# A hybrid decoder layer on one core: the last down tile split at token 256, and the closing norm's vectors in PSUM

## The reference

```python
x = layer_norm(ALPHA * x + merged @ w_out, ln1_g, ln1_b)
f = (jax.nn.silu(x @ w_ff_gate) * (x @ w_ff_up)) @ w_ff_down
x = layer_norm(ALPHA * x + f, ln2_g, ln2_b)
```

## Time and profile before

| what | value |
|---|---|
| median of three runs | 979.53 us (978.2, 979.53, 979.75) |
| the profiled execution, its own time | 978.52 us |
| its span, first to last instruction | 976.7 us |
| TensorE matmul busy | 937.5 us (96% of the span), granted clock 0.987 of full on average |
| VectorE busy | 612.2 us (63%) |
| ScalarE busy | 380.1 us (39%) |
| GpSimd busy | 368.5 us (38%) |
| DMA | 89.35 MB, mean 91 GB/s |

### The profile page before, as it was taken

The page is one execution under the profiler, slowest core; times in us unless marked ns, Lnnn a source line. Parts: engine busy times, 40 slices in busy tenths (PEclk is TensorE's granted clock), DMA queues, the critical chain, the costliest instruction groups (busy, mean ns, idle before and its releaser), DMA issues.

```text
span 976.7 us, 18914 instructions
## 1 busy us (share of the span) xinstructions
PE 937.5 (96%) x7382; PEld 932.4 (95%) x7382; DVE 612.2 (63%) x929; ACT 380.1 (39%) x593; POOL 368.5 (38%) x286
## 2 busy tenths in 40 slices
PE   6979999999999999999999999999999999999993
PEld 6979999999999999999999998999999999999992
DVE  2796979795302898543344689977878778321216
ACT  3423232324636333333222446555455457222211
POOL 3735565647354454444345453000000003433413
PEclk9989999999999999999999999999999999999996
DMA  8523232322322323322334230433433433432202
GB/s 240 152 63 96 86 95 86 86 65 75 97 66 66 98 66 96 97 84 78 97 101 125 66 87 1 130 87 98 117 86 89 125 86 101 139 93 86 60 1 92
DMA packets 166658, 89.35 MB, mean 91 GB/s; under 512 B 4634, under 2 KB 164674, under 8 KB 166609
## 3 DMA queue, kind: packets, MB, share of 16 engines
q1 hardware_dynamic: 164377, 87.75, 31.3%
q10 hardware_dynamic: 2232, 0.92, 0.4%
HBM read 85.49 MB, written 3.17 MB: 91 GB/s over the span
## 4 chain that ended last, share of the span: by engine, by line
PE 82%; DVE 13%; SPq 2%; issue 1%; ACT 1%; DMA 1%; DVEq 0%
PE main L1079 52%; PE main L1313 18%; PE main L1229 4%; PE aux L1313 3%; DVE aux L1547 2%; PE aux L1079 2%; PE aux L1065 1%; SPq L429 1%; DVE x_sum L1901 1%; DMA ln_tok<-in_ln_b 1%; DVE merged L1770 1%; DVE merged L1725 1%; DVE main L1722 0%; DVE glu_pad L1558 0%; DVE aux L1528 0%
## 5 line engine op out<-in xcount | busy, mean ns | idle before, releaser
L532 POOL TENSOR_TENSOR w_lo<-raw,w_hi 128x1024 fp32r<-128x1024 f32 (+1 forms) x128 | 280.6, 2196 | 554.6 <-ACT w_hi L654 552.5
L1079 PE MATMUL main<-x_hi,w_lo 128*128 128x272 f32 x1024 | 213.5, 290 | 6.5 <-DVE dch_pad L1572 5.0
L1079 PE MATMUL main<-x_hi,w_hi 128*128 128x272 f32 x1024 | 212.9, 289 | 0.0
L1079 PE MATMUL main<-x_lo,w_hi 128*128 128x272 f32 x1024 | 212.1, 289 | 0.0
L654 ACT ACTIVATE w_hi<-raw 128x1024 fp32r<-128x1024 f32 x128 | 135.2, 1058 | 146.2 <-PE main L1079 139.8
L1079 PEld LDWEIGHTS main<-x_hi,w_lo 128*128 128x128 f32 x1024 | 161.9, 189 | 7.2 <-POOL w_lo L532 5.2
L1079 PEld LDWEIGHTS main<-x_lo,w_hi 128*128 128x128 f32 x1024 | 161.8, 190 | 0.0
L1079 PEld LDWEIGHTS main<-x_hi,w_hi 128*128 128x128 f32 x1024 | 160.8, 190 | 0.0
L1079 PE MATMUL main<-y,w_hi 128*128 128x272 f32 x512 | 84.6, 287 | 0.0
L1547 DVE SCALAR_TENSOR_TENSOR aux<-glu_pad,miscT,aux 128x512 f32<-128x512 f32 x112 | 75.2, 751 | 0.0
L1079 PEld LDWEIGHTS main<-y,w_hi 128*128 128x128 f32 x512 | 72.1, 188 | 0.0
(11 more groups left out here) (366 smaller groups left out, 2128.4 us busy)
## 6 DMA issues: line engine op xcount, KB each, us to landing
raw<-in_w_in SPq DMA_DIRECT2D x64, 512.0 KB, 4.1
raw<-in_w_ff_gate SPq DMA_DIRECT2D x22, 512.0 KB, 4.0
raw<-in_w_ff_up SPq DMA_DIRECT2D x22, 512.0 KB, 5.0
raw<-in_w_branch SPq DMA_DIRECT2D x32, 256.0 KB, 3.5
raw<-in_w_ff_down SPq DMA_DIRECT2D x16, 512.0 KB, 4.0
raw<-in_w_out SPq DMA_DIRECT2D x8, 512.0 KB, 3.9
raw<-in_w_ff_down SPq DMA_DIRECT2D x8, 384.0 KB, 3.4
x_tok<-in_x_prompt SPq DMA_DIRECT2D x4, 512.0 KB, 6.4
```

The lines of the kernel that those rows point to most:

```text
L532: pool.tensor_tensor(w_lo[s][:, 0:n, :], raw[s][:, 0:n, :], w_hi[s][:, 0:n, :].bitcast(F32), ALU.subtract).then_inc(w_lo_ready, 1)
L1079: mm = pe.matmul(ps[:, h, :], w[s][:, k, :], x[:, h * HALF:(h + 1) * HALF], start=(first and k == 0 and j == 0), stop=(last and k == n - 1 ...
```

## The change

Two edits meet in the last 35 us.

*The split.* The last tile is made in two unequal parts, given by a table `LAST`: first tokens 256 to 544 (288 columns: token tiles 2, 3 and the samples), then tokens 0 to 256 (tiles 0 and 1). A new function `turn_last(n)` turns a part; that of the first part, with the samples, comes 12 matmuls into the second instead of 24. `half_unit` is no longer called here. The first residual step now writes back to the matmul's own PSUM bank and not to `S[2]`. VectorE takes `row_statistics(KD - 2)` ahead of the first residual, and finishes in another order: the samples and half of tile 2, the residual of the second part, the rest of tile 2, the second statistics, tile 0, the left half of tile 1. ScalarE and GpSimd take tile 3, and then the right half of tile 1. The output DMAs are in a new order.

*The vectors.* ScalarE copies `g_row` to `g_ps` (`main` banks 0 and 1) and `b_row` to `b_ps` (`aux` banks 2 and 3) once these banks are free, and `finish` reads `g_ps` and `b_ps`. GpSimd still reads `g_row` and `b_row`.

```diff
+        g_ps = main[:, 0:2, :].rearrange("p a n -> p (a n)")
+        b_ps = aux[:, 2:4, :].rearrange("p a n -> p (a n)")
+        LAST = ((2, NTILE + 1, 2 * P, NT), (0, 2, 0, 2 * P))
...
-                    (rows_ready, 1, o_x[:, 0, :], r_tok[:, 0, :]), (pool_rows, 2, o_x[:, 1, :], r_tok[:, 1, :]),
-                    (rows_ready, 2, o_x[:, 2, :], r_tok[:, 2, :]),
-                    (pool_rows, 4, o_x[:, 3, D // 2:D], r_tok[:, 3, D // 2:D]),
-                    (rows_ready, 3, o_s, rs_tok[:, :]),
-                    (rows_ready, 4, o_x[:, 3, 0:D // 2], r_tok[:, 3, 0:D // 2]))):
+                    (rows_ready, 1, o_s, rs_tok[:, :]), (rows_ready, 3, o_x[:, 2, :], r_tok[:, 2, :]),
+                    (pool_rows, 2, o_x[:, 3, :], r_tok[:, 3, :]), (rows_ready, 4, o_x[:, 0, :], r_tok[:, 0, :]),
+                    (pool_rows, 4, o_x[:, 1, D // 2:D], r_tok[:, 1, D // 2:D]),
+                    (rows_ready, 5, o_x[:, 1, 0:D // 2], r_tok[:, 1, 0:D // 2])):
...
-            for n, (j, cols) in enumerate(((1, slice(0, D)), (3, slice(D // 2, D)))):
+            for n, (j, cols) in enumerate(((3, slice(0, D)), (1, slice(D // 2, D)))):
...
+            act.wait_ge(row_vecs, 32)
+            act.wait_ge(tile_out[0], T_DOWN + KD // 2 + 1)
+            act.activation(g_ps, g_row[:, :], ACT.Copy).then_inc(vecs_copied, 1)
+            act.wait_ge(rows_out, KD - 1)
+            act.activation(b_ps, b_row[:, :], ACT.Copy).then_inc(vecs_copied, 1)
+            for n, (j0, j1, c0, c1) in enumerate(LAST):
+                act.wait_ge(rows_turned, KD + n)
+                ins = act.activation(r_tok[:, j0:j0 + 2, D - P:D],
+                                     aux[:, 1 - n, 0:2 * P].rearrange("p (j n) -> p j n", j=2), ACT.Copy)
+                if n == 0:
+                    ins = act.activation(rs_tok[:, D - P:D], aux[0:B * T, 1, 2 * P:3 * P], ACT.Copy)
...
+            def turn_last(n):
+
+                c0, c1 = LAST[n][2:]
+                pe.wait_ge(r_ready, 3 * KD + n)
+                pe.wait_ge(rows_out, KD - 2 + n)
+                for j in range(2):
+                    mm = pe.transpose(aux[:, 1 - n, j * P:j * P + P], S[1][:, c0 + j * P:c0 + j * P + P], ident[:, :])
+                if n == 0:
+                    mm = pe.transpose(aux[0:B * T, 1, 2 * P:3 * P], S[1][:, SEQ:NT], ident[:, :])
+                mm.then_inc(rows_turned, 1)
...
+                    for i in range(parts_):
+                        if n == 0 and k + i == DOWN_SPLIT[0]:
                             turn_rows(KD - 2)
+                        if n == 1 and k + i == 4:
+                            turn_last(0)
+                        xh, xl = h_hi(k + i)[:, c0:c1], h_lo[:, k + i, c0:c1]
+                        for t, (w, x) in enumerate(((w_l, xh), (w_h, xl), (w_h, xh))):
+                            mm = pe.matmul(main[:, 2 + n, 0:c1 - c0], w[:, i, :], x,
+                                           start=(k + i == 0 and t == 0), stop=(k + i == KF - 1 and t == 2))
+                    k += parts_
+                mm.then_inc(last_done, 1)
+            turn_last(1)
...
-                ve.scalar_tensor_tensor(S[2][:, cols], x_lo[:, KD - 1, cols].bitcast(F32), ALPHA,
-                                        main[:, 2 + h, 0:HALF], ALU.mult, ALU.add).then_inc(last_out, 1)
+                ve.scalar_tensor_tensor(bank, x_lo[:, KD - 1, c0:c1].bitcast(F32), ALPHA, bank,
+                                        ALU.mult, ALU.add).then_inc(last_out, 1)
...
-                after(link(ve.scalar_tensor_tensor(t, t, bn_mv[0:q, j, 0:1], g_row[0:q, cols],
+                after(link(ve.scalar_tensor_tensor(t, t, bn_mv[0:q, j, 0:1], g_ps[0:q, cols],
                                                    ALU.subtract, ALU.mult)))
-                ve.scalar_tensor_tensor(t, t, bn_rs[0:q, j, 0:1], b_row[0:q, cols], ALU.mult, ALU.add)\
+                ve.scalar_tensor_tensor(t, t, bn_rs[0:q, j, 0:1], b_ps[0:q, cols], ALU.mult, ALU.add)\
                   .then_inc(rows_ready, 1)
...
+            row_statistics(KD - 2)
             residual_last(0)
-            row_statistics(KD - 2)
             ve.wait_ge(bn_zero, 1)
-            last_statistics(0, 0, 2)
-            ve.wait_ge(row_vecs, 32)
+            last_statistics(0, 2, NTILE + 1)
+            ve.wait_ge(vecs_copied, 2)
+            finish(rs_tok[:, :], B * T, NTILE, slice(0, D))
+            finish(r_tok[:, 2, left], P, 2, left)
+            residual_last(1)
+            finish(r_tok[:, 2, right], P, 2, right)
+            last_statistics(1, 0, 2)
             finish(r_tok[:, 0, :], P, 0, slice(0, D))
-            ve.wait_ge(unit_done, U_END)
-            residual_last(1)
-            last_statistics(1, 2, NTILE + 1)
-            finish(r_tok[:, 2, :], P, 2, slice(0, D))
-            finish(rs_tok[:, :], B * T, NTILE, slice(0, D))
-            finish(r_tok[:, 3, 0:D // 2], P, 3, slice(0, D // 2))
+            finish(r_tok[:, 1, left], P, 1, left)
```

More of the change, by code:

```diff
@@ L1404, in _ @@
             pe.wait_ge(tile_out[1], T_DOWN + (KD - 1) // 2 + 1)
-            for h in range(2):
+            for n, (j0, j1, c0, c1) in enumerate(LAST):
                 k = 0
-                for part, n in enumerate(DOWN_SPLIT):
+                for part, parts_ in enumerate(DOWN_SPLIT):
                     u = U_END - 3 + part
-                    if h == 0:
+                    if n == 0:
                         pe.wait_ge(w_lo_ready, u + 1)
-                    mm = half_unit(w_hi[u % RING], w_lo[u % RING],
-                                   [(h_hi(k + j), h_lo[:, k + j, :]) for j in range(n)],
-                                   main[:, 2 + h, 0:HALF], h, first=(part == 0), last=(part == 2))
-                    k += n
-                    if h == 1:
-                        mm.then_inc(unit_done, 1)
-                    elif part == 2:
-                        mm.then_inc(last_half, 1)
-                    if part == 0:
-                        if h == 0:
-                            turn_rows(KD - 2)
-                        else:
-                            pe.wait_ge(r_ready, 3 * KD)
-                            pe.wait_ge(rows_out, KD - 2)
-                            for j in range(2):
-                                mm = pe.transpose(aux[:, 1, j * P:j * P + P], S[1][:, j * P:j * P + P],
-                                                  ident[:, :])
-                            mm.then_inc(rows_turned, 1)
@@ L1429, in _ @@
-            pe.wait_ge(r_ready, 3 * KD + 1)
-            pe.wait_ge(rows_out, KD)
-            for j in range(2, NTILE):
-                pe.transpose(aux[:, 1, j * P:j * P + P], S[1][:, j * P:j * P + P], ident[:, :])
-            pe.transpose(aux[0:B * T, 3, 0:P], S[1][:, SEQ:NT], ident[:, :]).then_inc(rows_turned, 1)
+                    w_h, w_l = w_hi[u % RING], w_lo[u % RING]
+                    for i in range(parts_):
+                        if n == 0 and k + i == DOWN_SPLIT[0]:
+                            turn_rows(KD - 2)
+                        if n == 1 and k + i == 4:
[4 more added lines that the diff above has]
+                                           start=(k + i == 0 and t == 0), stop=(k + i == KF - 1 and t == 2))
```

37 lines of the change are left out of this document (15 added, 22 removed).

## The result

| | before | changed |
|---|---|---|
| median | 978.6 us (6 runs, 975.33 to 979.75) | 972.61 us (6 runs, 970.02 to 974.82) |
| ratio | 1 | 0.994, 95% interval 0.9916 to 0.9964 |
| profiled execution | 978.52, span 976.7 | 974.82, span 973.0 |

The kernel is faster by 0.6%, in the direction and by the way that were forecast, but 972.61 lies 0.19 under the low end of the range (972.8).

The account below looks back on a forecast made before the run. VectorE was taken to bound the last 17.3 us, 3.1 of it waiting for GpSimd. VectorE's end -5.34 and DMA queue +0.44 gave -4.9, from 979.0 to 974.1 us; range 972.8 to 976.5.

Parts of the forecast that it names:

- So I take both as free of each other: Closing norm: VectorE's finish with a PSUM vector and GpSimd don't wait for each other; 1.28 us per instruction of 1024 columns.
- Rival 1: Closing norm: VectorE and GpSimd still wait for each other with vectors in PSUM; 980.7 us, chance 0.02.
- I take nothing for it: VectorE's residual and finishing instructions: reading PSUM instead of SBUF costs no extra time.
- Rival 4: VectorE's eleven instructions newly reading PSUM cost a little more, 0.2 us in all; 974.3 us, chance 0.10.
- The copies: ScalarE's two vector copies into PSUM fit its idle time; 0.8 to 3.0 us for both, cost nothing.
- Rival 2: Last tile's second part: 256-column matmuls run at another rate, 0.23 us each; 980.9 us, chance 0.04.
- -5.34 + 0.44 = -4.9: Whole span: VectorE's end 5.34 us earlier, queueing of the last output DMAs 0.44 later, so 4.9 less.
- with 0.03 between: VectorE's finishing instructions: a gap of 0.03 us between one and the next.
- +1.3 = 971.8: Output DMA tail: the last bytes end at 970.49 and the span 1.3 us later, at 971.8.
- down 1.3 for the runs' spread (978.2 against 979.5): Low side of the forecast range: 1.3 us under 974.1 for run spread and no DMA queue, giving 972.8.
- Rival 5: Last tile: an unseen wait eats the new order's gain, only 3.1 us of GpSimd waiting saved; 975.9 us, chance 0.06.
- rival 3: Output DMA tail: the last three transfers go one after another, 1.7 us later; 975.8 us, chance 0.10.

Follow-up runs that it names:

- E4: Changed kernel without GpSimd's four closing-norm instructions; 28.86 us from the last tile's first matmul to the span's end, against 28.93.
- E7: Changed kernel with the second part's residual ahead of the left half of tile 2; 29.95 us from the last tile's first matmul to the span's end.
- E13: Kernel before plus two small VectorE writes that nobody reads; 33.87 us from the last tile's first matmul to the span's end, against 34.60.
- E1: Kernel before with only the vectors moved to PSUM, its split, order and residual kept; median 974.26 us, ratio 0.9939.
- E3: Kernel before without GpSimd's four closing-norm instructions; 31.18 us from the last tile's first matmul to the span's end, against 34.60.
- E2: Changed kernel with the vectors left in SBUF and no copies, new split and order kept; median 978.4 us, ratio 0.9986.

## Why the prediction was right, and where it wasn't

- **"So I take both as free of each other":** right. E4 puts what is left at 0.07 of stretch. Rival 1 is refuted.
- **"I take nothing for it" (PSUM reads):** right. On 1024 columns 1.27 and 1.28 against 1.28, on 512 0.73 to 0.75 against 0.73 and 0.75. Rival 4 doesn't show in any of the eleven. Nor does the rule of the Trainium skill, "VectorE: DVE Perf Modes", section "The TRN2 errata" (an estimated 0.065 more each); the measurement decides.
- **The copies:** 1.01 and 1.00, between the bounds 0.38 and 1.52, and hidden.
- **The matmuls:** end at 17.42, predicted 17.42. Rival 2 fell: 256 columns take 0.117.
- **VectorE to the first finishing:** starts at 13.93, predicted 13.81; the residual at 17.86 against 17.97. The wait that the new order makes is there (0.44 after the last matmul, predicted 0.55), and E7 shows that to do without it is worse.
- **The sum, "-5.34 + 0.44 = -4.9":** this is the step that failed. The stretch lost 5.67. The mechanism was right, and two terms of the sum had the wrong size, by 0.45 and 0.32:
- **"with 0.03 between":** VectorE's end lies at 25.92, predicted 26.37, so 0.45 too late. I had put 0.03 between all instructions. Where one has no wait of its own it starts some 0.08 before its predecessor's end (968.46 against 967.26 + 1.28 = 968.54), so a pair of 512 columns takes 1.43 to 1.44 instead of 1.51. The earlier trace rows showed it: 971.09 + 1.27 = 972.36, and the next starts at 972.29.
- **"+1.3 = 971.8" (from the last bytes to the end):** predicted 3.33 from VectorE's end, measured 3.01, so 0.32 too long. The queue itself is right: E13, whose code packet comes early, has a tail of 2.52, the changed kernel 3.01, so +0.49 against the predicted +0.44. But the 1.3 of the kernel before held 0.37 that goes with its late code packet, and the changed kernel, with two more VectorE instructions, lost it. I took a row of one kernel as a constant of the chip. That the edit moved the packet was luck.
- **The range:** with both terms as measured the forecast is 974.1 - 0.77 = 973.3 and the low end 972.0, and 972.61 is inside; one of the two alone would have done for the 0.19. The other 0.7 down to 972.61 is scatter of runs, for which "down 1.3 for the runs' spread (978.2 against 979.5)" left little room: my 979.0 for the kernel before came from four executions, and its median beside the experiments lies between 978.6 and 979.8. Three runs showed 1.5 of spread; six of the changed kernel have 4.8, and 17 of the kernel before, run beside E1, have 6.2 (975.56 to 981.8). A spread read from three runs was made into a bound.
- **Rival 5** is refuted by the stretch (5.67 off, and 4.94 by the account below, not 3.1), and rival 3 by the tail.

One more thing that I had read wrongly: part of VectorE's idle 1.56 before the second statistics. TensorE's timeline of the kernel before, and of E13:

```profile
961.66 0.69 PE L1432 MATMUL aux<-ident,scr 128*128 128x128 f32 x2 [2.24 <-DVE scr L1983]
```
```profile
960.10 0.44 PE L1432 MATMUL aux<-ident,scr 128*128 128x128 f32 x2 [2.22 <-DVE scr L1983]
```

Two stretches of the kernel before, and the one of E13 (PEclk is the third number from the end):

```profile
961.00:962.00 1.00, 0.34 (x2) 0.34 (x3) 0.61 (x1) 0.00 (x0) 0.92 (x2) 0.76 0.26 102
962.00:963.00 1.00, 0.56 (x3) 0.08 (x1) 0.00 (x0) 0.40 (x2) 1.00 (x1) 0.50 0.00 0
```
```profile
960.00:961.00 1.00, 0.55 (x3) 0.27 (x3) 0.06 (x3) 0.32 (x2) 1.00 (x1) 1.00 0.02 8
```

The granted clock falls to 0.50 of full (1.2 GHz) in the one and stays at 1.00 (2.4 GHz) in the other, after the same idle time; E1 and E3, idle for 1.18 and 1.01, kept it too. So 0.36 of the kernel before's stretch (0.69 + 0.23 for the three transposes against 0.44 + 0.12) is the clock's fall, which came in one profile and not in the other. Of the 5.67 then, 0.36 is that, 0.37 goes with the code packet, and 33.87 - 28.93 = 4.94 is the design: 5.43 on VectorE, less 0.49 for the queue of stores. E1 and E2 split it. The vectors alone are worth 3.29 - 0.36 = 2.93, and the order on top of them 2.38 - 0.37 = 2.01. The order alone, 34.36 with its code packet early, is 0.49 longer than E13: while the vectors lie in SBUF it is a small loss.
